# Stick-breaking attention: the softplus of most steps is split into a rounded part and a remainder before it is summed over later keys

## The reference, cut to what matters

```
z    = q @ k.T * 64**-0.5                       # per head, query t, key s
strict = s < t
log_beta      = log_sigmoid(z)
log_one_minus = where(strict, log_sigmoid(-z), 0)
tail = reverse_cumsum_over_keys(log_one_minus) - log_one_minus
A    = where(strict, exp(log_beta + tail), 0)
out  = A @ v
```

## Time and profile before

| | us |
|---|---|
| median of three runs | 2509.17 |
| lowest and highest | 2508.76, 2509.76 |
| the profiled execution, its own time | 2507.71 |
| its span, first to last instruction | 2505.9 |
| outside the span | 1.8 |

### The profile page before, as it was taken

The page is one execution under the profiler, slowest core; times in us unless marked ns, Lnnn a source line. Parts: engine busy times, 40 slices in busy tenths (PEclk is TensorE's granted clock), DMA queues, the critical chain, the costliest instruction groups (busy, mean ns, idle before and its releaser), DMA issues. The chain is left out here.

```text
span 2505.9 us, 35916 instructions
## 1 busy us (share of the span) xinstructions
PE 2429.7 (97%) x13179; PEld 1933.0 (77%) x13179; DVE 1500.7 (60%) x2193; ACT 1050.2 (42%) x2024; POOL 1074.8 (43%) x830
## 2 busy tenths in 40 slices
PE   7999999999999999999999988899999999999998
PEld 6788556878888888887788877764787888888887
DVE  3231652585554567883553245568259888888777
ACT  3200662453333334464233245368255444444444
POOL 4443356165544543332454553253435444543321
PEclk9999999999999999999999999999999999999999
DMA  4110113213322359871111200000421332336975
GB/s 137 47 50 22 51 35 135 101 43 118 109 97 100 120 184 352 278 265 56 47 51 51 55 14 2 4 16 1 161 75 59 116 111 89 110 113 242 340 268 217
DMA packets 165490, 278.31 MB, mean 111 GB/s; under 512 B 16597, under 2 KB 64960, under 8 KB 165320
## 3 DMA queue, kind: packets, MB, share of 16 engines
q1 hardware_dynamic: 160384, 259.15, 30.8%
q10 hardware_dynamic: 4936, 16.90, 1.7%
HBM read 218.81 MB, written 57.18 MB: 110 GB/s over the span
## 5 line engine op out<-in xcount | busy, mean ns | idle before, releaser
L1371 POOL TENSOR_TENSOR ring_lo_conv<-operand_sum_conv,ring_hi_conv 128x512 fp32r<-128x512 f32 x140 | 199.1, 1435 | 257.8 <-ACT ring_hi_conv L1622 257.8
L1371 POOL TENSOR_TENSOR ring_lo<-operand_sum,ring_hi 128x512 fp32r<-128x512 f32 x140 | 190.3, 1370 | 244.7 <-ACT ring_hi L1622 244.7
L115 POOL TENSOR_TENSOR w_hi<-w_raw,zero 128x512 fp32r<-128x512 f32 x92 | 107.0, 1163 | 269.6 <-PE bank L178 199.4
L178 PE MATMUL bank<-xt_hi,w_hi 128*128 128x512 f32 x384 | 149.5, 389 | 0.0
L178 PE MATMUL bank<-xt_hi,w_lo 128*128 128x512 f32 x384 | 149.4, 389 | 0.0
L178 PE MATMUL bank<-xt_lo,w_hi 128*128 128x512 f32 x384 | 149.4, 389 | 0.0
L1495 PE MATMUL bank<-xt_hi,ring_hi_conv 128*128 128x512 f32 x352 | 137.6, 391 | 2.0 <-DVE hidden_raw_conv L1948 1.3
L1495 PE MATMUL bank<-xt_hi,ring_hi 128*128 128x512 f32 x352 | 137.6, 391 | 1.2 <-DVE hidden_raw L1938 0.6
L1497 PE MATMUL bank<-xt_hi,ring_lo_conv 128*128 128x512 f32 x352 | 137.0, 389 | 0.0
L1497 PE MATMUL bank<-xt_hi,ring_lo 128*128 128x512 f32 x352 | 137.0, 389 | 0.0
L1496 PE MATMUL bank<-xt_lo,ring_hi 128*128 128x512 f32 x352 | 137.0, 389 | 0.0
(11 more groups left out here) (611 smaller groups left out, 6844.7 us busy)
## 6 DMA issues: line engine op xcount, KB each, us to landing
down_in<-in_w_down_dram SPq DMA_DIRECT2D x130, 256.0 KB, 4.7
down_in_conv<-in_w_ffn_down_dram SPq DMA_DIRECT2D x130, 256.0 KB, 4.7
up_raw<-in_w_gate_up_dram SPq DMA_DIRECT2D x88, 256.0 KB, 3.7
up_raw_conv<-in_w_ffn_up_dram SPq DMA_DIRECT2D x88, 256.0 KB, 3.6
down_in<-hidden_between SPq DMA_DIRECT2D x76, 256.0 KB, 3.8
down_in_conv<-hidden_between_conv SPq DMA_DIRECT2D x76, 256.0 KB, 3.8
w_raw<-in_w_mix_in_dram SPq DMA_DIRECT2D x64, 256.0 KB, 2.7
hidden_between<-hidden_sums SPq DMA_DIRECT2D x11, 1024.0 KB, 4.3
```

Of the source, the lines that this page charges most:

```text
L115: pool.tensor_tensor(m.w_hi[:, u, :], m.w_raw[:, u, :], zeros, ALU.add).then_inc(m.hi_done, 1)
L178: mm = pe.matmul(m.psum[b][:, :], lhs, rhs, start=k == 0 and i == 0, stop=k == KD - 1 and i == 2)
L1371: pool.tensor_tensor(shaped(ring_lo[SLOT[e]][:, :], e), source(e), shaped(ring_hi[SLOT[e]][:, :].bitcast(F32), e), ALU.subtract).then_inc( ...
```

## The change: what it does

In 18 of the 24 steps, softplus is no longer given to PE in float32. DVE writes a rounded copy "softplus_hi" in fp32r, POOL the remainder "softplus_lo", and PE uses each in one matmul with a rounded copy of the triangular matrix. The steps are 2 to 7 and 10 to 21 (the list "parted"): not the narrowest ones (128 columns) and not the last two.

- DVE: two copies more in each of the 18 steps, right behind softplus(p). They wait for the softplus result and for sums two steps before, which read the same plane.
- POOL: two subtractions more in each of these steps (soft_low). They stand in POOL's list in front of the later_lo pair of the same step. The two xt_lo instructions move from before the attention to behind soft_low(4) and soft_low(5). One small instruction makes tri_r.
- PE: in these steps sums has two fp32r matmuls in place of one float32 matmul, and waits for the remainder.
- ACT: the logarithm of step p waits, in addition, for the remainder of step p - 2, which reads the plane that it overwrites.

```diff
+    all_r, tri_r = m.at("minus_ones_r", [P, P], 185.25, F32R), m.at("tri_r", [P, P], 194.5, F32R)
+    sp_hi, sp_lo = m.at("softplus_hi", [P, 4, HALF], 24, F32R), m.at("softplus_lo", [P, 4, HALF], 48, F32R)
+    parted = [p for p in range(2, L - 2) if steps[p][1] - 4 * steps[p][0] <= 2]
+    def parts(p, i):
+        return 2 * parted.index(p) + i + 1
...
@@ gpsimd
+            pool.wait_ge(made, 4)
+            pool.tensor_tensor(tri_r[:, :], tri[:, :], m.zero[:, 0:1].to_broadcast([P, P]), ALU.add).then_inc(made, 1)
+            def soft_low(p):
+                if p in parted:
+                    for i, (u, h, bank, g, b) in enumerate(units(p)):
+                        c0 = cols(g, b)
+                        pool.wait_ge(soft_hi, parts(p, i))
+                        pool.tensor_tensor(sp_lo[:, h, c0:HALF], sp[:, h, c0:HALF], sp_hi[:, h, c0:HALF].bitcast(F32),
+                                           ALU.subtract).then_inc(soft_lo, 1)
...
-            for k in range(2):
-                pool.wait_ge(sc_hi, k + 1)
-                pool.tensor_tensor(m.xt_lo[:, k, :], sc[:, k, :], m.xt_hi[:, k, :].bitcast(F32), ALU.subtract)
+            for p in range(SPLIT_FROM):
+                soft_low(p)
+                if p in (4, 5):
+                    pool.wait_ge(sc_hi, p - 3)
+                    pool.tensor_tensor(m.xt_lo[:, p - 4, :], sc[:, p - 4, :], m.xt_hi[:, p - 4, :].bitcast(F32), ALU.subtract)
             for p in range(SPLIT_FROM, L):
+                soft_low(p)
                 for u, h, bank, g, b in units(p):
...
@@ tensor, sums(p)
+                    if p in parted:
+                        pe.wait_ge(soft_lo, parts(p, u - 2 * p))
+                        pe.matmul(m.psum[bank][:, c0:HALF], tri_r[:, :], sp_hi[:, h, c0:HALF], start=False, stop=False,
+                                  skip_group_check=True)
+                        mm = pe.matmul(m.psum[bank][:, c0:HALF], tri_r[:, :], sp_lo[:, h, c0:HALF], start=False, stop=False,
+                                       skip_group_check=True)
+                    else:
...
@@ vector, end of softplus(p)
+                if p in parted:
+                    for i, (u, h, bank, g, b) in enumerate(units(p)):
+                        c0 = cols(g, b)
+                        dve.wait_ge(soft, u + 1)
+                        if p > 1:
+                            dve.wait_ge(summed, u - LAG + 1)
+                        dve.tensor_copy(sp_hi[:, h, c0:HALF], sp[:, h, c0:HALF]).then_inc(soft_hi, 1)
...
@@ scalar, in front of the logarithm in logs(p)
+                    if p - 2 in parted:
+                        act.wait_ge(soft_lo, parts(p - 2, u - 2 * p))
```

More of the change, by code:

```diff
@@ L3068, in read_stage @@
     acc_hi, acc_lo = m.at("later_hi", [P, 4, HALF], 152, F32R), m.at("later_lo", [P, 4, HALF], 160, F32R)
-    all_r = m.at("minus_ones_r", [P, P], 185.25, F32R)
+    all_r, tri_r = m.at("minus_ones_r", [P, P], 185.25, F32R), m.at("tri_r", [P, P], 194.5, F32R)
+    sp_hi, sp_lo = m.at("softplus_hi", [P, 4, HALF], 24, F32R), m.at("softplus_lo", [P, 4, HALF], 48, F32R)
+    soft_hi, soft_lo = m.sem("sb_soft_hi"), m.sem("sb_soft_lo")
     gn = ROW["w_gdn_norm_2"]
@@ L3153, in _ @@
                         pe.matmul(m.psum[h][:, 0:P], kd[:, h, c, :], vn[:, h, :], start=True, stop=True).then_inc(pe_s, 1)
-            pe.wait_ge(made, 6)
+            pe.wait_ge(made, 7)
             pe.wait_ge(dve_s, 8 * NT - 4)
@@ L3178, in sums @@
                     pe.wait_ge(soft, u + 1)
-                    mm = pe.matmul(m.psum[bank][:, c0:HALF], tri[:, :], sp[:, h, c0:HALF], start=False, stop=False,
-                                   skip_group_check=True)
+                    if p in parted:
[5 more added lines that the diff above has]
+                    else:
+                        mm = pe.matmul(m.psum[bank][:, c0:HALF], tri[:, :], sp[:, h, c0:HALF], start=False, stop=False,
+                                       skip_group_check=True)
                     if b != 4 * g + 3:
```

## The result

The changed kernel takes 2552.89 us (2552.12 to 2553.81 in four runs) against 2509.25 us for the kernel before (2508.76 to 2509.76): a ratio of 1.0175, with a 95% interval of 1.0161 to 1.0189. It is 43.6 us slower. The forecast was 2562, in a range from 2535 to 2580.

The account below looks back on a forecast made before the run. PE and the loop over DVE and ACT were taken as about level. Copies, lock, POOL's queue and smaller terms summed to +53.2 us on 2507.7, giving 2560.9, or 2562 as median, in a range of 2535 to 2580.

Parts of the forecast that it names:

- copies: DVE's two rounded copies per parted step, ahead of the next add_later and cap, lengthen its loop: +10.9 us.
- lock, steps up to 15: POOL's two remainders per step hold up DVE's SBUF-to-SBUF additions and copies through the shared ports: +23.6 us.
- moved xt_lo: Leaving iteration 0 saves about 2.3 us; holding DVE's additions in iterations 3 and 4 costs 2.33 each: net +2.3.
- end of the first half: output_low(6)'s 1.26 us wait for ACT, which waits for PE, goes once DVE is later: -1.1 us.
- iteration 15: Four POOL instructions in a row behind soft_hi(16) delay add_later(15); 9.9 us against 6.07 before: +3.8.
- iterations 16 to 19: POOL's four instructions, an addition, softplus and copies run in series: 7.4 us against 4.68, four times, +11.0.
- iteration 20: No copies behind it, but later_lo(22) is issued between the two additions; 8.65 us against 4.68 to 4.78: +3.9.
- tail: PE will have caught up, so sums(23) starts about 4.4 us behind cap(23) in place of 5.6: -1.2.
- The alternation: Up to step 15, DVE's four short instructions alternate with POOL's two long ones, both in the path, 1.25 us each at 512 columns.
- POOL's queue from step 16 on: add_later(p + 1) waits for later_lo(p + 1), queued behind soft_low(p + 1); four POOL instructions in series take 5.0 us.
- PE's saving: Two fp32r matmuls for one float32 in sums save 15.0 us, absent from the sum since PE no longer ends last.
- The rival of the clock: PE's granted clock falls to half speed as PE idles in the attention: about +9 us, 2571 us; chance 0.17.

Follow-up runs that it names:

- Copies alone: Changed kernel with no remainder made: nothing new on POOL, PE uses the rounded copy in both fp32r matmuls; 2524.30 us, ratio 1.0067.
- later_lo first: Changed kernel with POOL doing later_lo(p) ahead of the remainder of softplus from step 16 on; 2546.53 us, ratio 1.0161.
- Second part alone: Changed kernel with only steps 16 to 21 parted, steps 2 to 15 as in the kernel before; 2528.61 us, ratio 1.0084.
- Made, not used: Changed kernel still making copies and remainders, but PE does one float32 matmul on softplus in every step and waits for no remainder; 2554.43 us, ratio 1.0188.
- both runs with PE's saving: Kernel before with softplus written rounded and used twice by PE, no copies or remainders: 2506.36 us; also with cap(p + 2) ahead of add_later(p): 2503.31 us.
- Remainders behind the additions: Changed kernel with one more wait: in steps 2 to 15 POOL begins remainders only after DVE finishes add_later(p - 1); 2541.17 us, ratio 1.0133.
- Repaired: Changed kernel with remainders waiting for DVE's additions up to step 15, later_lo ahead from step 16, xt_lo back before the attention; 2534.85 us, ratio 1.0100.
- six runs named above: Six runs with a low granted clock at the next stage's start; from its first matmul to the end 741.0 to 742.1 us, others 739.4 to 739.9.
- The order alone: Kernel before with DVE doing cap(p + 2) ahead of add_later(p) up to step 15, nothing split; 2510.95 us, ratio 1.0013.

## Why the prediction was right, and which sizes were off

The mechanism was right: DVE's loop lengthened by copies, by the lock and by POOL's queue, with PE's part lying beside it. The sizes were a little too large. The forecast lengthened the attention by 53.2 us; the stage grew by 47.8. The other 4 us of the distance between 2562 and 2553 are no merit or fault of the sum: the profiled execution started the stage 1.8 us earlier and was 0.5 us shorter behind it, and its time lay 0.2 us above the median, where the profile before lay 1.5 below. By its own terms, each from the start times of DVE's instructions before and after:

| term | predicted | measured |
|---|---|---|
| copies | 10.9 | 10.5 |
| lock, steps up to 15 | 23.6 | 18.8 |
| moved xt_lo | 2.3 | 1.8 |
| end of the first half | -1.1 | -0.1 |
| iteration 15 | 3.8 | 3.1 |
| iterations 16 to 19 | 11.0 | 10.1 |
| iteration 20 | 3.9 | 3.5 |
| tail | -1.2 | 0.1 |
| sum | 53.2 | 47.8 |

**The copies.** 0.42 us was read between a 128-column and a 1024-column copy, and 0.42 it is (L3299: two in 0.76, and 0.67 to the next start). "Copies alone" bears it out: 7.0 us up to iteration 14, where these lengths add up to 7.1.

**The lock** is shown, by three runs from different sides: remainders moved in time (-15.7 us of stage), moved to the engine that was held up (-18.8, with the steps from 16 on, xt_lo and the tail in it), and made without use by PE (no change). The term was mis-sized. I let DVE lose POOL's whole 1.25 us; it lost 1.48 - 0.41 = 1.07 and 1.29 - 0.21 = 1.08. That is 0.17 to 0.19 less per instruction of POOL, on 24 of them 4.3 us; in iteration 1 one of the two fell beside cap, 0.5 more. My own rows had it: add_later's 1.79 in place of 0.68 is 1.11 lost to an instruction of 1.28, and the copy's 2.38 in place of 0.22 is 2.16 lost to one of 2.36. I wrote "the whole of the other's instruction" beside them. The same fits iterations 15 to 20: iteration 15, where four of POOL's instructions hold DVE up, came 0.7 us short of its term.

**The alternation** of the four short additions with POOL's two long ones came out as drawn, and xt_lo in the place named: in iteration 3 its 2.35 us stand beside an addition of 128 columns that takes 2.46. It costs 2.2 us there and 2.2 in iteration 4, where I had 2.33 each. What iteration 0 got back was 2.5, since before both of its copies were held, not one: two took 2.89 us, and 0.35 after.

```profile
1662.59 2.89 DVE L3278 COPY later<-softplus 128x128 f32<-128x128 f32 x2
```

```profile
1674.23 2.35 POOL L3145 TENSOR_TENSOR xt_lo<-sc,xt_hi 128x1024 fp32r<-128x1024 f32 x1
1674.27 2.46 DVE L3314 TENSOR_TENSOR later<-later,softplus 128x128 f32<-128x128 f32 x1
```

**POOL's queue from step 16 on** is shown by "later_lo first", and its share by "Second part alone", 19.4 us of stage.

**Two small terms came to nothing.** The 1.26 us wait at the end of the first half did not go. I had put it down to PE. But it stands in "Made, not used", where PE waits for no remainder, in "Copies alone" and in "Second part alone" as well:

```profile
1704.67 0.69 DVE L3317 TENSOR_TENSOR xt_lo<-bank,xt_hi 128x512 fp32r<-128x512 f32 x1 [1.26 <-ACT xt_hi L3392]
```

In all of them xt_lo starts 1.73 or 1.74 us behind cap(9), as before. ACT has the exponentials and logarithms of step 9 in its list ahead of xt_hi, and these wait for that cap: the wait belongs to the loop of DVE and ACT, and moves with DVE.

The tail gained nothing either: sums(23) came 5.75 us behind cap(23), as before (5.63). The step itself was sound. In "Made, not used", "Second part alone" and both runs with PE's saving it came 4.25 or 4.26 behind, the 4.4 that I had said, and the stage ended 1.4 us sooner behind cap(23); in the runs where the granted clock was low there ("Copies alone", "Remainders behind the additions", "later_lo first", "Repaired") it came 5.40 to 5.65 behind. What took the gain away is, by the traces, PE's clock. In the changed kernel's profile it was at the lower level just there, and in "Second part alone" it wasn't; of each the window and the scores of step 23 in it:

```profile
1794.00:1796.00 2.00, 2.00 (x5) 0.51 (x4) 2.00 (x3) 1.64 (x3) 2.00 (x2) 0.50 0.00 0
1794.01 2.08 PE L3185 MATMUL bank<-sqk 64*128 64x512 f32 x4
```

```profile
1769.00:1771.00 2.00, 1.95 (x9) 0.80 (x10) 2.00 (x2) 1.32 (x3) 2.00 (x3) 1.00 0.00 0
1769.74 1.13 PE L3185 MATMUL bank<-sqk 64*128 64x512 f32 x4
```

The scores took 0.95 us more, and the values behind them 1.64 in place of 1.08: together the 1.5 us by which the two tails differ.

**PE's saving** stood nowhere in the sum, and alone it is worth 1 us of stage. Only together with a shorter order on DVE does a part of it show.

**The rival of the clock** was half right: the granted clock did fall, to a mean of 0.82 in the stage, and against my argument that the gaps were too short. That argument was wrong: PE's gaps grew up to 4.1 us (the longest wait in the lines of its profile), longer than the 2.73 I had compared them with. But up to cap(23) the low stretches cost nothing that shows, since the other terms fill the whole growth, and where cap did wait for scores, 0.77 us, the loop over POOL was no longer for it. They cost 1.5 us in the tail. I had priced them at 9 us. In the six runs named above a low stretch fell behind the stage, and the rest of the program was 1 to 3 us longer. No run held the clock fixed, so these prices are read from traces alone.

Left open: why "The order alone" is slower by 0.1%. Behind the first cap DVE waits 7.5 us for scores in its profile, and not at all before; and 1.1 us of the profile's excess lie behind the stage, where the granted clock was 0.66 from 1766 to 1770 us against 1.00 before. No run took the two apart.

## What to carry to other kernels

Before work is moved to GpSimd, look for what VectorE does at the moment the work is released: in this kernel an addition or copy from SBUF to SBUF then waited for nearly the whole of each GpSimd instruction (1.07 us of 1.23 at 512 columns), and cap, which reads PSUM, kept its 1.28 us for two. If they must share, a wait that pushes GpSimd beside the PSUM operations can be worth more than an early start, as it was here. An engine that is busy all the time isn't the bound if another is level with it: make the saving alone, at no cost, before paying for it.

## What the runs showed of the hardware that was not expected

- Undisturbed, in "Remainders behind the additions", GpSimd's subtractions start 1.23 us after each other at 512 columns, 0.96 at 384 and 0.68 at 256. In the changed kernel each held VectorE's SBUF-to-SBUF instructions for 1.07, 0.80 and 0.53 to 0.55 us: some 0.15 us less.
- VectorE's rounding copy, already under way when GpSimd starts, isn't slowed: 0.76 us for two with a subtraction beginning 0.50 us after the first. If GpSimd is there first, two take up to 2.71.
- With PE busy for three quarters of the stage, its granted clock went up and down between the two levels, to means of 0.53 to 1.00 in stretches of 10 us.
- What a low stretch costs depends on where it falls: nothing that shows in a loop that other engines hold (7.84 to 7.86 us an iteration throughout), 1.5 us in the tail; and where it lay at the start of the next stage, with PE busy for 3.77 of 4 us, the rest of the program took 1 to 3 us longer.
